# Side blocks turned around the sample rows, and the last root ahead of the side copies, at the two norms before the up projections

## The reference

```python
xp = layer_norm(DN_ALPHA * xp + mp, ln_mix_g[l], ln_mix_b[l])     # 512 prompt rows
xs = layer_norm(DN_ALPHA * xs + ms, ln_mix_g[l], ln_mix_b[l])     # 64 sample rows
fp, cbp = conv_ffn(xp, buf0, ffn_w_up[l], ffn_conv_w[l], ffn_conv_b[l], ffn_w_down[l])
fs, cbs = conv_ffn(xs, state_ffn_conv[l], ...)
...
def conv_ffn(x, buf, w_up, conv_w, conv_b, w_down):
    u = x @ w_up                                   # 1024 -> 2 * 2816
    ext = concatenate([buf, u], axis=1)            # two earlier rows of each sequence in front
    y = conv_b + sum(conv_w[j] * ext[:, j:j + T] for j in range(3))
    val, gate = y[..., :D_FF], y[..., D_FF:]
    return (silu(gate) * val) @ w_down, ext[:, -2:]
```

## Time and profile before

| | |
|---|---|
| median of 3 runs | 1561.87 us (1561.52 to 1563.39) |
| the profiled execution's own time | 1563.41 us |
| its span, first to last instruction | 1561.3 us |
| TensorE busy | 1479.7 us, 95% of the span |
| VectorE busy | 909.5 us, 58% |
| ScalarE busy | 562.7 us, 36% |
| mean granted TensorE clock | 0.978 of full |

### The profile page before, as it was taken

How to read it: one execution, slowest core, us unless ns; L and a number is a source line. 1 busy time by engine, 2 the same in 40 slices (tenths; PEclk the granted TensorE clock), 3 DMA queues, 4 the chain that set the end, 5 groups by cost and what they waited for, 6 DMA issues and landing times.

```text
span 1561.3 us, 24279 instructions
## 1 busy us (share of the span) xinstructions
PE 1479.7 (95%) x9372; PEld 1312.1 (84%) x9372; DVE 909.5 (58%) x1734; ACT 562.7 (36%) x1062; POOL 60.4 (4%) x90
## 2 busy tenths in 40 slices
PE   7999898889999999999999999989899999999995
PEld 6888676679999999778798888768899999998784
DVE  4644354386666666635731877765766666664546
ACT  3222276333333333432323433541333333343231
POOL 1002200010000000000100100110100000000000
PEclk9999999989999999999988999989999999999998
DMA  5235324533233222534412211361122222214211
GB/s 196 88 101 178 114 66 119 168 80 83 81 82 84 82 82 71 203 140 144 138 52 79 81 54 55 113 210 55 55 82 81 81 81 81 81 54 132 82 67 61
DMA packets 153911, 153.56 MB, mean 98 GB/s; under 512 B 12374, under 2 KB 123222, under 8 KB 153382
## 3 DMA queue, kind: packets, MB, share of 16 engines
q1 hardware_dynamic: 149938, 139.54, 29.3%
q0 software_dynamic: 3904, 13.07, 2.4%
HBM read 140.76 MB, written 21.91 MB: 104 GB/s over the span
## 4 chain that ended last, share of the span: by engine, by line
PE 86%; DVE 7%; ACT 3%; issue 2%; DMA 1%; POOL 1%; SPq 0%; ACTq 0%; DVEq 0%; POOLq 0%
PE ps L702 70%; PE ps L713 5%; PE ps L683 4%; PE ps L1069 1%; PE ps L777 1%; PE ps L811 1%; ACT w_hi L1209 1%; DVE x_reg L1796 1%; DVE x_reg L1800 1%; ACT attn_side L1195 1%; DVE w_lo L1583 1%; PE ps L990 1%; POOL w_lo L2186 1%; DVE x_reg L1778 1%; DVE ln_stats L1785 1%
## 5 line engine op out<-in xcount | busy, mean ns | idle before, releaser
L702 PE MATMUL ps<-xh_reg,w_hi 128*128 128x288 f32 x1552 | 465.2, 300 | 8.6 <-DVE xl_reg L1590 5.1
L702 PE MATMUL ps<-xl_reg,w_hi 128*128 128x288 f32 x1552 | 460.8, 297 | 0.0
L702 PE MATMUL ps<-xh_reg,w_lo 128*128 128x288 f32 x1552 | 460.8, 297 | 0.0
L702 PE MATMUL ps<-w_hi,xh_reg 128*128 128x512 f32 x768 | 308.0, 401 | 7.9 <-DVE xl_reg L1837 3.4
L702 PEld LDWEIGHTS ps<-xh_reg,w_hi 128*128 128x128 f32 x1552 | 295.1, 190 | 11.0 <-issue 6.2
L702 PE MATMUL ps<-w_hi,xl_reg 128*128 128x512 f32 x768 | 302.1, 393 | 0.0
L702 PE MATMUL ps<-w_lo,xh_reg 128*128 128x512 f32 x768 | 301.8, 393 | 0.0
L702 PEld LDWEIGHTS ps<-xl_reg,w_hi 128*128 128x128 f32 x1552 | 295.2, 190 | 0.0
L702 PEld LDWEIGHTS ps<-xh_reg,w_lo 128*128 128x128 f32 x1552 | 294.9, 190 | 0.0
L1583 DVE TENSOR_TENSOR w_lo<-raw,w_hi 128x2048 fp32r<-128x2048 f32 (+1 forms) x51 | 111.4, 2184 | 244.1 <-ACT w_hi L1209 244.1
L702 PEld LDWEIGHTS ps<-w_hi,xh_reg 128*128 128x128 f32 x768 | 145.9, 190 | 40.4 <-issue 7.2
(11 more groups left out here) (204 smaller groups left out, 1462.3 us busy)
## 6 DMA issues: line engine op xcount, KB each, us to landing
raw<-in_ffn_w_up SPq DMA_DIRECT2D x88, 512.0 KB, 4.9
raw<-in_ffn_w_down SPq DMA_DIRECT2D x40, 512.0 KB, 4.6
raw<-in_attn_w_in SPq DMA_DIRECT2D x24, 512.0 KB, 4.8
raw<-in_gla_w_in SPq DMA_DIRECT2D x24, 512.0 KB, 4.5
out_swa_s<-in_state_swa_kv SPq DMA_DIRECT2D x16, 496.0 KB, 6.5
x_reg<-in_x_prompt SPq DMA_DIRECT2D x8, 512.0 KB, 7.4
raw<-in_gla_w_out SPq DMA_DIRECT2D x8, 512.0 KB, 4.8
out_swa_p<-arena POOLq DMA_DIRECT2D x18, 128.0 KB, 3.3
```

The source lines that it names most:

```text
L702: mm = pe.matmul(out, lhs(i, a), rhs(i, b), start=first and i == 0 and a + b == 0, stop=last and i == ks - 1 and a == 1)
```

## The change

At both norms it splits the side turns. The 22 transposes of half 0 stay ahead of the samples' turn, those of half 1 go behind it, and both write banks of their own (7 and 4) with semaphores of their own, `side_turned` and `side_taken`. ScalarE takes the root of the samples first, then copies half 0, then the samples, then half 1; ahead of the first copy of the up projection it waits for both side copies. The batch numbers lose the two places that the side turns had.

```diff
+SIDE_BANKS = (7, 4)
...
-        BATCH_LN1 = BATCH_LN0 + TURNS_X + 2
+        BATCH_LN1 = BATCH_LN0 + TURNS_X
...
-            def turn_sides(l):
+            def turn_side(l, v):
 
                 pe.wait_ge(side_loaded, 48 * (l + 1))
-                for v in range(2):
-                    turn([(j * SIDE, side[0:SIDE, (v * NJ + j) * P:(v * NJ + j + 1) * P]) for j in range(NJ)])
+                for j in range(NJ):
+                    mm = pe.transpose(ps[:, SIDE_BANKS[v], j * SIDE:(j + 1) * SIDE],
+                                      side[0:SIDE, (v * NJ + j) * P:(v * NJ + j + 1) * P], ident[0:SIDE, 0:SIDE])
+                mm.then_inc(side_turned, 1)
...
                 elif m == 2:
                     if stage % 2 == 0:
-                        turn_sides(stage // 2)
+                        turn_side(stage // 2, 0)
                     after_ln(stage, [4])
-                    pe.wait_ge(turned_out, first_batch + TURNS_X + (0 if stage % 2 else 2))
+                    if stage % 2 == 0:
+                        turn_side(stage // 2, 1)
+                    pe.wait_ge(turned_out, first_batch + TURNS_X)
                     lo_here(first_batch, TURNS_X)
...
                     elif t == 3:
                         take_x(3)
-                        if stage % 2 == 0:
-                            take_sides()
+                    elif stage % 2:
+                        take_x(4)
                     else:
+                        take_side(stage // 2, 0)
                         take_x(4)
-
-            def take_sides():
-                for v in range(2):
-                    take(feat[:, v, :, :].rearrange("p j r -> p (j r)"), lambda b: b[:, 0:NJ * SIDE])
+                        take_side(stage // 2, 1)
+
+            def take_side(l, v):
+                act.wait_ge(side_turned, 2 * l + v + 1)
+                act.activation(feat[:, v, :, :].rearrange("p j r -> p (j r)"), ps[:, SIDE_BANKS[v], 0:NJ * SIDE],
+                               ACT.Copy).then_inc(side_taken, 1)
 
             def ffn(l):
                 act.wait_ge(turned_out, batch.n)
+                act.wait_ge(side_taken, 2 * (l + 1))
```

More of the change, by code:

```diff
@@ L382, in build_program @@
         side_loaded = sem("side_loaded")
+        side_turned = sem("side_turned")
+        side_taken = sem("side_taken")
         pads_zero = sem("pads_zero")
@@ L452, in build_program @@
         LO_BATCHES = ([b for b in range(TURNS_X)]
-                      + [b0 + b + (2 if b0 in (BATCH_LN0, BATCH_LN2) and b >= 8 else 0)
-                         for b0 in (BATCH_LN0, BATCH_LN1, BATCH_Y, BATCH_LN2) for b in range(TURNS_X)])
+                      + [b0 + b for b0 in (BATCH_LN0, BATCH_LN1, BATCH_Y, BATCH_LN2) for b in range(TURNS_X)])
         def state_place(n):
```

## The result

The changed kernel takes 1554.11 us (median of 7, 1549.04 to 1555.09) against 1561.87 (median of 7, 1559.56 to 1563.39): ratio 0.9942, 95% interval 0.9929 to 0.9956. That is 7.8 us less, where 8.0 were forecast. Measured twice more, the ratio was 0.9934 (0.9921 to 0.9946) and 0.9946 (0.9931 to 0.9960).

What follows compares the result with a forecast made beforehand. TensorE, busy 95% of the span, bounds the kernel, losing time to waits and low clock at both norms. Earlier restarts give 7.3 us and the clock 0.7: 8.0 off 1561.87 makes 1553.9, range 1549.0 to 1557.2.

Steps and rivals of the forecast that it cites:

- The root was late, and its wait goes: Samples' norm, layer 0: root taken at 338.8, norm done at 341.46, so TensorE's wait from 342.90 to 345.19 is gone.
- The restart, 3.6 us after m = 1, a gain of 7.3 us in both layers: Start of m = 2: 343.6 against 347.33 in layer 0, 1115.7 against 1119.37 in layer 1; gains 3.7 and 3.65 us.
- My sign for it: Profile after, if right: products of m = 2 start 3.5 to 3.7 us after those of m = 1 end.
- What lies under half 1: Layer 0: samples' copy and rest end at 343.5 under side half 1, whose turns end at 343.6 and set the restart.
- The clock still falls in both blocks and returns 0.7 us: After both restarts: 0.50 clock for 3.4 to 5.4 us, costing 2.2 us a layer against 2.55; chance 0.50, 1553.9.
- each rival of the clock: At the two blocks: clock falls in both (0.50, 1553.9), in one (0.27, 1551.7) or in none (0.13, 1549.5).
- falls in one block only: Clock falls at one of the two blocks and holds at the other: gain 10.2 us, 1551.7; chance 0.27.
- hold in both: Clock stays up at both blocks: gain 12.4 us, 1549.5; chance 0.13.
- The lower bound of the gain, 4.5 us: Restart gain in both layers if the clock falls during the samples' turn and half 1's 22 transposes double: 1557.4.
- The second weight unit stays hidden: Up projection, layer 0: unit ready at 348.5, TensorE asks for it at 350.1; slack of 1.6 us stays.
- The slower rival: Weight unit ready more than 8.0 us after 348.5, after a side copy's unseen 9 us wait a layer: 1564; chance 0.04.
- the one of another wait: Second weight unit or side copies come late, 4 us in both layers: gain 3.2 us, 1558.7; chance 0.06.

Runs made afterwards that it cites:

- the root alone: Kernel before with only the samples' root moved ahead of the side copies, all 44 side turns staying ahead of the samples' turn: 1555.88 us, ratio 0.9964.
- few-turns kernel: Changed kernel with 2 of the 22 transposes in each side half, the others left out: 1550.97 us, ratio 0.9933.
- both halves ahead of m = 1: Changed kernel with both side halves turned ahead of the products of m = 1: 1554.42 us, ratio 0.9951.
- the split alone: Changed kernel with the samples' root put back behind the copy of side half 0: 1560.63 us, ratio 0.9994.

## Why the prediction was right, and where it was not

- *The root was late, and its wait goes.* Right, shown by the profile after (root and L1806 start together at 337.76) and by the root alone, which gives 5.7 us.
- *The restart, 3.6 us after m = 1, a gain of 7.3 us in both layers.* Right in layer 1 (3.58 us). In layer 0 the term was mis-sized: 4.39 us, 4.56 and 4.17 in the two later traces. I took side half 1 at full clock, "since in both blocks the fall came after the last side turn", and kept the doubled turns only as a bound. In all three traces of the changed kernel the clock fell under half 1 in layer 0, which cost 0.5 to 0.9 us. The sum of both layers is 6.5 us, not 7.3. My sign for it, products of m = 2 starting 3.5 to 3.7 us after those of m = 1, failed in layer 0.
- *What lies under half 1.* I timed the samples' copy and rest from the rows before, 2.0 us from the start of their turn. With nothing in the way they take 1.8 (341.22 to 343.03 in the few-turns kernel; 340.48 to 342.14 and 0.14 here). So the turns bound the restart, and by more than the 0.1 us I had.
- *The clock still falls in both blocks and returns 0.7 us.* Right in direction; it returned 1.1 in the profiled executions, mostly in layer 1. The rows I took it from were one draw: at the norm between the layers, with the same wait, the clock was at 0.50 in the trace before and at 1.00 in the first trace after.
- *One price for each rival of the clock.* Time and mean clock of an execution do go together. Over 18 executions of the changed kernel in three sets, 11 have a mean clock of 0.981 and a mean time of 1554.3, and 7 have 0.984 and 1550.7. Over 39 of the kernel before (0.977 to 0.982) the mean is 1561.5. But the two blocks don't decide which: the trace in which the clock fell in both (1551.67 us) is one of the 0.984, and that in which it held in layer 1 (1554.67, the rival "falls in one block only") is the slowest of its set. In the three traces the one at 0.984 parts from the two at 0.981 between the blocks (735.6 us against 738.8 and 738.7). The prediction's prices took the clock outside its two blocks as it was in one trace; only its range left room for it. In no trace of the changed kernel did it hold in both.
- *Readings and sums.* "Layer 1's clock outlasted 1.5 us of products and 3 us of turns" isn't what the rows show: it outlasted 2.9 us of turns and 2.3 of waiting. 144 products at full clock take 19.54 us and not 19.41, so the low stretches before cost 4.8 us and not 5.1. The lower bound of the gain, 4.5 us, gives 1557.4, and the range ends at 1557.2.
- *The second weight unit stays hidden.* Right: ready at 346.10 + 2.29 = 348.39 against my 348.5, and TensorE's products run through (144 in a row).
- *The slower rival and the one of another wait* have nothing for them in the trace.
- The miss on distance (0.8) and the surplus on clock (0.4) nearly cancel. Executions of the changed kernel spread over 6 us, so a median within 0.2 us of the forecast is luck; the 7.6 us of the two blocks against 8.0 are the better measure of how good it was.

The Trainium skill says on the page "TensorE: Matmul & The Clock Gate", Part 4, that the full clock doesn't engage for transposes, since they don't count as busy in the same way. The runs agree in part. The clock fell with TensorE busy in turns without a pause (both halves ahead of m = 1, layer 0), but in layer 1 of the same trace it stayed at 1.00 through 3.7 us of them, and it fell 0.6 us after a restart with products between the strings of turns. That turns and useful products differ at equal length was not settled in times.

## What to carry to other kernels

On an engine that runs its instructions in the order of its program, as ScalarE does in these rows, a tiny instruction on which another engine waits (a root of 64 numbers, 0.3 us) belongs ahead of every copy that itself waits for something: here it stood behind two side copies, and VectorE waited 3.6 us for it at the norm of layer 0 and TensorE 2.3 behind that. Work moved to fill a wait on TensorE should be priced at both clocks. The low clock can also come under a long string of transposes without any wait (once here, 4.1 us of them). Moving a string in between products, at the same amount of work, lowered the median by 4.5 us and the mean by 3.6 on the one chip where both ran; about 2.7 us of it were seen in the blocks themselves. And before a difference between two profiles is put down to a change, add up the stretches that the change doesn't touch: here they held 4 of 11.7 us.

## What the runs showed of the hardware

A string of 22 transposes of 20 by 128 took 1.47 us at a granted clock of 1.00 and 1.99 to 2.38 where the clock had fallen to 0.50 on the way. At 0.50 all through they took 2.46 (the split alone), 1.7 times as long. The products of 288 columns stood 0.13 us apart at 1.00 and 0.24 at 0.50, 1.8 times. The granted clock fell without any idle time on TensorE (both halves ahead of m = 1, layer 0). The same program in the same place had the clock fall in one execution and hold in the next (the changed kernel's layer 1: 3.4 us low, 3.4, none), and at the norm between the layers, which no change touches, it was at 0.50 in one trace and at 1.00 in another, worth 2.4 us. The times of executions follow their mean clock: in the changed kernel the means of those at 0.981 and those at 0.984 lie 3.6 us apart.
